# Earlier splitting of two output projections' weight blocks, and three of each expert's loads in unequal pieces

## The reference

```python
for layer in range(2):
    # shift, scale and gate rows of each sublayer: silu(c) @ ada_w[layer] + ada_b[layer]
    hx, hc = modulate(x, ...), modulate(ctx, ...)
    if layer == 0:
        yx, yc = fourier_window_mixer(hx, hc, mix_in_w, mix_out_w, win_sink, ...)
    else:                                     # no ctx output is needed
        yx, yc = diff_mixer(hx, hc, diff_qkv_w, diff_out_w, diff_lambda, diff_subln_g, ...)
    x = x + g1x * rmsnorm(yx)                 # ctx likewise in layer 0
    # layer 0: swiglu with 2816 hidden; layer 1: 8 experts of 3584 hidden, two per token
    x = x + g2x * rmsnorm(channel(modulate(x, ...)))
```

## Time and profile before

| | |
|---|---|
| time, median of 3 runs | 1702.79 us (1701.99 to 1703.03) |
| the profiled execution | 1705.14 us, of which 1703.4 us span |
| TensorE busy | 1620.9 us, 95% |
| VectorE, ScalarE busy | 525.9 us, 400.5 us |
| read from HBM | 471.36 MB, 277 GB/s over the span |
| chain that ended last | PE 89%, DVE 5%, DMA 2%, ACT 2%, SPq 1%, issue 1% |

### The profile page before, as it was taken

One profiled execution on the slowest core, in us unless ns is written; L12 is line 12 of the kernel. 1 busy time (PEld: TensorE's weight loads), 2 busy tenths in 40 slices (PEclk: granted clock), 3 DMA queues, 4 the chain that ended last, 5 costly groups with the idle time before them and its releaser, 6 DMA issues.

```text
span 1703.4 us, 31517 instructions
## 1 busy us (share of the span) xinstructions
PE 1620.9 (95%) x13979; PEld 970.4 (57%) x13979; DVE 525.9 (31%) x829; ACT 400.5 (24%) x724; POOL 34.4 (2%) x70
## 2 busy tenths in 40 slices
PE   5999889999999989997899999999999999999996
PEld 2855578878788877866644434454453444544432
DVE  3417367665533366357500010100101010020012
ACT  3227353211232253348300101011011100010101
POOL 1000100010000000000000000000000000000000
PEclk9999999999999999999799999999999999999998
DMA  9461725676623324103999999999999999999995
GB/s 368 175 195 60 252 77 174 197 254 231 217 91 122 113 80 134 40 0 133 362 377 374 378 408 408 413 406 411 408 409 411 394 411 405 410 412 399 410 397 226
DMA packets 140559, 474.61 MB, mean 279 GB/s; under 512 B 11176, under 2 KB 35144, under 8 KB 121984
## 3 DMA queue, kind: packets, MB, share of 16 engines
q1 hardware_dynamic: 137344, 467.64, 71.8%
q0 software_dynamic: 3072, 4.88, 1.0%
HBM read 471.36 MB, written 1.13 MB: 277 GB/s over the span
## 4 chain that ended last, share of the span: by engine, by line
PE 89%; DVE 5%; DMA 2%; ACT 2%; SPq 1%; issue 1%; DVEq 0%; ACTq 0%
PE ps L1139 85%; DMA w_raw<-in_ada_w_dram 1%; SPq L585 1%; DMA w_raw<-in_expert_out_w_dram 1%; PE ps L1644 1%; DVE w_lo L1759 1%; DVE work L1828 1%; PE ps L1322 1%; ACT p L953 0%; ACT w_hi L725 0%; DVE row_max L2094 0%; PE ps L1636 0%; DVE p L2120 0%; DVE h_t L1817 0%; DVE work L2026 0%
## 5 line engine op out<-in xcount | busy, mean ns | idle before, releaser
L1139 PE MATMUL ps<-w_hi,h_t 128*128 128x512 f32 (+1 forms) x960 | 295.9, 389 | 13.5 <-DVE h_t L1817 5.4
L1139 PE MATMUL ps<-h_t,w_hi 128*128 128x512 f32 (+1 forms) x768 | 223.3, 376 | 6.2 <-DVE h_t L1817 6.2
L1139 PEld LDWEIGHTS ps<-w_hi,h_t 128*128 128x128 f32 x960 | 181.6, 192 | 51.4 <-DVE w_lo L1942 4.1
L1759 DVE TENSOR_TENSOR w_lo<-w_raw,w_hi 128x2048 fp32r<-128x2048 f32 x57 | 130.6, 2292 | 219.3 <-ACT w_hi L725 219.0
L1139 PE MATMUL ps<-w_lo,h_t 128*128 128x512 f32 (+1 forms) x480 | 186.4, 388 | 0.0
L1139 PE MATMUL ps<-w_raw,h_te 128*32 128x512 f32 (+2 forms) x2224 | 178.4, 475 | 1.5 <-ACT silu_g L1053 0.8
L725 ACT ACTIVATE w_hi<-w_raw 128x2048 fp32r<-128x2048 f32 x57 | 109.0, 1914 | 290.2 <-PE ps L1139 289.8
L1139 PE MATMUL ps<-w_moe,h_te 128*32 128x512 f32 (+2 forms) x2256 | 170.5, 456 | 0.0
L1139 PEld LDWEIGHTS ps<-h_t,w_hi 128*128 128x128 f32 x768 | 142.0, 192 | 33.8 <-issue 9.2
L1139 PE MATMUL ps<-work 128*32 128x512 f32 (+6 forms) x1232 | 147.7, 485 | 8.3 <-ACT p L953 3.7
L2282 DVE TENSOR_TENSOR residual<-silu_g,ps 128x512 f32<-128x512 f32 (+1 forms) x20 | 12.4, 621 | 438.5 <-ACT silu_g L1056 418.0
(11 more groups left out here) (285 smaller groups left out, 1281.2 us busy)
## 6 DMA issues: line engine op xcount, KB each, us to landing
w_raw<-in_expert_in_w_dram SPq DMA_DIRECT2D x68, 1024.0 KB, 18.8
w_moe<-in_expert_in_w_dram SPq DMA_DIRECT2D x62, 1024.0 KB, 18.6
work<-in_expert_in_w_dram SPq DMA_DIRECT2D x53, 1024.0 KB, 18.2
w_raw<-in_ada_w_dram SPq DMA_DIRECT2D x48, 1024.0 KB, 5.4
w_raw<-in_expert_out_w_dram SPq DMA_DIRECT2D x37, 1024.0 KB, 17.9
w_moe<-in_expert_out_w_dram SPq DMA_DIRECT2D x36, 1024.0 KB, 18.2
work<-in_expert_out_w_dram SPq DMA_DIRECT2D x33, 1024.0 KB, 17.9
w_raw<-in_ffn_in_w_dram SPq DMA_DIRECT2D x44, 512.0 KB, 5.0
```

Of the source, the lines that this page charges most:

```text
L1139: return pe.matmul(out_, l, r, start=first, stop=last, skip_group_check=True)
L1759: dve.tensor_tensor(WLO[:, b % SPL, :], WRAW[:, slot_w[b], :], WHI[:, b % SPL, :].bitcast(F32), ALU.subtract).then_inc(lo_done, 1)
```

## The change

Three groups of edits:

1. `raw_order` takes blocks 5 and 6 directly behind block 4. ScalarE and VectorE split block 5 before they wait for block 3's product, and block 6 before they wait for block 4's; nothing is split in the units of the first attention. VectorE's `ada_rows(2)` moves behind `output0(15)`.
2. Blocks 54 and 55 are split while TensorE works on the last column group of q, k, v (n = 5); nothing is split in the units of the second attention. The heads of tile 0 are transposed (banks 2 and 3) ahead of the probabilities of unit 15, and ScalarE evacuates them in unit 14; the values of unit 15 move into the output projection, before its third row group; the heads of tile 1 go to banks 4 and 5. SP issues expert loads 5 to 8 first, without waiting for the scores.
3. The second output block of each of an expert's first three steps (b = 1: 3 of its 42 loads, 24 in all) is loaded by three transfers, of partitions 0 to 111, 112 to 119 and 120 to 127. Each raises the semaphore by 16, and TensorE waits for all three.

```diff
-    raw_order = [("ada", a) for a in range(8)] + [("w", r) for r in range(5)]
-    raw_order += [("ada", a) for a in range(8, 20)] + [("w", 5), ("w", 6)]
-    raw_order += [("ada", a) for a in range(20, PE_ADA)] + [("w", r) for r in range(7, B_FFNIN + 3)]
+    raw_order = [("ada", a) for a in range(8)] + [("w", r) for r in range(B_MIXOUT + 2)]
+    raw_order += [("ada", a) for a in range(8, PE_ADA)] + [("w", r) for r in range(B_MIXOUT + 2, B_FFNIN + 3)]
...
+    def moe_uneven(n):
+        kind, s_, b = ROUND[n][:3]
+        return kind == "out" and s_ < STEPS - 1 and b == 1
+
     def moe_parts(n):
-        return 2 if ROUND[n][:2] == ("in", STEPS - 1) else 1
+        return 2 if ROUND[n][:2] == ("in", STEPS - 1) else 3 if moe_uneven(n) else 1
...
+    HEAD_BANK = (2, 4)
+    UNEVEN = ((0, P - 16), (P - 16, P - 8), (P - 8, P))
...
-                sp.dma_start(w, rows.rearrange("(p j) n -> p j n", j=2)).then_inc(done, 16)
+                rows = rows.rearrange("(p j) n -> p j n", j=2)
+                for lo, hi in UNEVEN if moe_uneven(n) else ((0, P),):
+                    sp.dma_start(w[lo:hi], rows[lo:hi]).then_inc(done, 16)
...
-                sp.wait_ge(scores, U0 + U1)
-                for n in range(RING0):
-                    if n == 3:
+                for n in [5, 6, 7, 8, 0, 1, 2, 3, 4] + list(range(9, RING0)):
+                    if n == 0:
+                        sp.wait_ge(scores, U0 + U1)
+                    elif n == 3:
                         sp.wait_ge(pv_done, U0 + U1)
...
         act.activation(F_N, ps[:, 0:4, :], ACT.Copy).then_inc(f_copied, 1)
+        hi_upto(B_MIXOUT + 1)
         act.wait_ge(used, B_MIXIN + 4)
...
         ins.then_inc(q_ctx, 1)
+        hi_upto(B_MIXOUT + 2)
         act.wait_ge(used, B_MIXIN + 5)
...
-            if u in (13, 15):
-                hi_upto(B_MIXOUT + (u - 11) // 2)
...
             hi_upto(min(B_QKV + 2 * n + 2 + SPL, B_DOUT))
+            if n == 5:
+                hi_upto(B_DOUT + 2)
             act.wait_ge(used, B_QKV + 2 * n + 2)
...
-            if 13 <= u < U1 - 1:
-                hi_upto(B_DOUT + u - 12)
...
-        act.wait_ge(lam_dve, 2)
-        heads_hi(0)
+            if u == U1 - 2:
+                act.wait_ge(lam_dve, 2)
+                heads_hi(0)
+
         output1(U1 - 1)
...
+            if u == U1 - 1:
+                pe.wait_ge(exps, U0 + U1 - 1)
+                head_transposes(0)
             pe.wait_ge(prob_scaled, U0 + u + 1)
...
-        head_transposes(0)
-        values1(U1 - 1)
-        linear(B_DOUT, ZT, [(0,), (1,)], range(0, 8, 2), before=heads_split, between={6: late_columns})
+        linear(B_DOUT, ZT, [(0,), (1,)], range(0, 8, 2), before=heads_split,
+               between={2: lambda: values1(U1 - 1), 6: late_columns})
...
```

More of the change, by code:

```diff
@@ L964, in output1, with heads_hi @@
                            accum_out=SS[:, u:u + 1]).then_inc(o_raw, 1)
+        def heads_hi(t):
+            for b in range(2):
+                act.wait_ge(o_tr, 2 * t + b + 1)
+                act.activation(ZT[:, 0, 4 * b:4 * b + 4, P * t:P * t + P],
+                               ps[:, HEAD_BANK[t] + b, :].rearrange("p (h q) -> p h q", h=4), ACT.Copy,
+                               scale=GSUB[:, 1:2]).then_inc(z_hi, 1)
         exps1(0)
@@ L1461, in values1, with head_transposes @@
             ins.then_inc(pv_done, 1)
+        def head_transposes(t):
+            for b_ in range(2):
+                pe.wait_ge(o_norm, 2 * t + b_ + 1)
+                for hh in range(4):
+                    h = 4 * b_ + hh
+                    ins = pe.transpose(ps[:, HEAD_BANK[t] + b_, hh * P:hh * P + P], OA[:, t, h * P:(h + 1) * P], ID[:])
+                ins.then_inc(o_tr, 1)
         for u in range(U1):
@@ L1475, in _ @@
                 values1(u - 1)
-        def head_transposes(t):
-            for b_ in range(2):
-                pe.wait_ge(o_norm, 2 * t + b_ + 1)
-                for hh in range(4):
-                    h = 4 * b_ + hh
-                    ins = pe.transpose(ps[:, 2 * t + b_, hh * P:hh * P + P], OA[:, t, h * P:(h + 1) * P], ID[:])
-                ins.then_inc(o_tr, 1)
         def late_columns():
@@ L1959, in _ @@
         lo_upto(B_MIXIN + 2 + SPL)
+        lo_upto(B_MIXOUT + 1)
         dve.wait_ge(used, B_MIXIN + 4)
@@ L1963, in _ @@
         dve.sem_inc(q_x, 1)
+        lo_upto(B_MIXOUT + 2)
         dve.wait_ge(used, B_MIXIN + 5)
@@ L2009, in _ @@
                 output0(u - 1)
-            if u in (13, 15):
-                lo_upto(B_MIXOUT + (u - 11) // 2)
+        output0(U0 - 1)
         ada_rows(2)
-        output0(U0 - 1)
         lo_upto(B_MIXOUT + 2 + SPL)
@@ L2079, in _ @@
                 lam_whole()
+            if n == 5:
+                lo_upto(B_DOUT + 2)
             dve.wait_ge(used, B_QKV + 2 * n + 2)
@@ L2108, in heads_lo @@
                 dve.scalar_tensor_tensor(out=ZT[:, 1, 4 * b:4 * b + 4, P * t:P * t + P],
-                                         in0=ps[:, 2 * t + b, :].rearrange("p (h q) -> p h q", h=4),
+                                         in0=ps[:, HEAD_BANK[t] + b, :].rearrange("p (h q) -> p h q", h=4),
                                          scalar=GSUB[:, 1:2],
@@ L2130, in _ @@
                 combine1(u + 1)
-            if 13 <= u < U1 - 1:
-                lo_upto(B_DOUT + u - 12)
             if u == 11:
```

## The result

| | median, us | ratio to before, 95% interval |
|---|---|---|
| before | 1702.39 (4 runs, 1701.57 to 1703.03) | |
| changed | 1824.38 (4 runs, 1813.88 to 1838.72) | 1.072 (1.0655 to 1.0785) |

The forecast was 1683.0 in a range from 1678 to 1700. The kernel is 122 us slower. That is the side of rival (a), and beyond its price.

A forecast was written before the change was run, and what follows sets the result against it. PE was taken as the bound, with DMA also full in the experts. Span 1703.4 - 8.3 - 6.0 - 5.5 = 1683.6 us, plus 1.7 around it 1685.3 as profiled, so median 1683.0; range 1678 to 1700.

The forecast's parts named there:

- rival (a): Uneven loads in the experts: narrow pieces slow the stream, costing 50 to 55 us, 1739 to 1743 in all; chance 15%.
- Part 1: End of the first attention: two PE waits shortened and the clock restored, 8.3 us saved, between 5 and 9.
- the terms (3.26, 2.0 and 1.3): Before the first output projection: wait for scaled probabilities 3.26 us, wait for the last `h_t` 2.0, clock on PE's work 1.3.
- the clock's term: From the last microsecond before 190 us to 196: full clock instead of 0.78 saves some 1.7 us.
- The assumption that it was to support: First attention's end: TensorE, kept fed, is not throttled, as in 130:176 us at clock 1.00; the clock terms rest on it.
- Part 2: End of the second attention: 4.83 + 3.0 - 1.3 - 0.5 = 6.0 us saved, between 3.5 and 7.
- the new wait of 1.3 us: Second output projection: PE waits for unit 15's values, evacuated and normalised, before tile 1's heads; 0 to 1.7 us, taken as 1.3.
- the 4.83 us: End of the second attention: PE's wait for VectorE's `p`, behind the splits of blocks 54 and 55, goes entirely.
- Part 3: Uneven expert loads: relieving eight DMA engines cuts PE's load waits in the tail by 5.5 us, between 0 and 6.8.
- I take the value of the shape nearest to the 112-partition piece, no penalty: Uneven expert loads: narrow pieces priced at zero, like a 128-partition piece at 379 to 440 GB/s, not 64 partitions at about 215.
- wide pieces of the next can fill what a narrow one leaves idle: Argument against rival (a): the queue holds several loads, so later wide pieces use what a narrow piece leaves idle.
- The relief: Expert loads: eight engines carry seven rows instead of eight, 7.7 us less each, offsetting instruction packets assumed on them.

The follow-up runs named there:

- the added loads: Six groups of full, narrow and strided loads, data thrown away, added on idle DMA engines to the changed kernel without uneven loads: 1689.07 us in one execution.
- parts 1 and 2 alone: The changed kernel with `moe_uneven` returning False, so no uneven loads, against the kernel before: 1689.56 us, ratio 0.9917.
- 112 and 16: The changed kernel with its 24 uneven blocks in two pieces, of 112 and 16 partitions, against the kernel before: 1811.36 us, ratio 1.0655.

## Why the prediction was wrong

- **Part 1, -8.3 us forecast.** Right in the time, 8.9, and a little over the high end of 9 between marks, 9.6. Ahead of the output projection's start 6.8 were gained where the terms (3.26, 2.0 and 1.3) make 6.6, and the wait is 0.70 for 0.7. Behind it 2.8 were gained, where the clock's term was 1.7. That the start of 181.09 is 1.2 earlier than the forecast 182.3 is luck: in that execution the first transposes already start 1.0 sooner (122.78 for 123.80). One row was misread: in 130:176 PE is busy 43.56 of 46 us, and 46.00 is the length of the stretch. The assumption that it was to support held all the same, with 13.30 of 14 us busy at clock 1.00. The dip a tenth of the way in isn't in the slices of the earlier trace rows either, which have one near the middle; it is the 0.85 and 0.78 of the earlier trace rows. The splits were hidden: VectorE's idle time of 7.19 us is 4.76 now, the split inside it.

```profile
85.74 2.29 DVE L1770 TENSOR_TENSOR w_lo<-w_raw,w_hi 128x2048 fp32r<-128x2048 f32 x1
92.79 0.35 DVE L1929 TENSOR_TENSOR work<-ps,tables 128x64 f32<-128x64 f32 x2 [4.76 <-PE ps L1148]
```

- **Part 2, -6.0 us.** Right: 5.6 in the time and 6.8 between marks; the new wait of 1.3 us is 1.30. The forecast of no wait for `p` came true for the 4.83 us; one of 1.06 stayed.
- **Parts 1 and 2 count in full** at the end: right. Alone they make 1689.56; the forecast's terms make 1688.5.
- **Part 3, -5.5 us.** Wrong, by 140 us. The step that failed is "I take the value of the shape nearest to the 112-partition piece, no penalty". The only rows of a transfer with fewer than 128 partitions said half the rate, and the 112-partition piece was put on the other side because its number is near 128. It runs at 0.76 of the rate by itself, 0.7 us too slow, and the two small pieces got no term at all in the sum, though by themselves they cost up to 1.8 us. I had worked out 0.6 us a block as the point from which the sum turns. In the stream the measured term is 5.6 us a block, 135 us in all, in place of a gain of 5.5.
- **Rival (a)** had the mechanism and the sign, at 15%, and a price of 2.1 to 2.3 us a block. Alone the pieces measure up to 2.5, so the size was right for idle engines, by luck: it took the rate of 64 partitions for the whole megabyte, but 112 partitions lose much less than that (0.7) and the small pieces the rest. In the stream it is 5.6, and the rate fell to 351 GB/s, not to the 380 that I gave as its sign. What I set against it, "wide pieces of the next can fill what a narrow one leaves idle", is the opposite of what happened: whole loads are slowed too (5711 slow packets, at most 3072 of them in uneven blocks).
- **The relief** rested on a cause (instruction packets on certain engines) that the rows only allowed. That cause stays unshown; what the added loads do show is that a transfer of 8 partitions ends with eight completions (and one update at its issue) and one of 112 with 16, as the sum took it. The most that the tail offered was 6.8 us against a known risk of 50, so even a fair chance of (a) made part 3 a bad bet.

The version that beats both kernels is parts 1 and 2 alone, 1689.56 us.

## What to carry to other kernels

Where the DMA engines are the second limit, a transfer is a choice of partitions before it is a number of bytes. Cut a load by columns, or into even and odd partitions; here every cut that had a run of neighbouring partitions, 24 blocks of it, cost 5.1 to 5.7 us a block, and small strided pieces 1.4 to 1.7. Price a new shape by the nearest row that has its property (fewer than all partitions), not its size, and when the gain is capped by a small wait and the loss by a whole stream, take the loss as the forecast unless a row excludes it. A saving ahead of a stream that follows PE counts in full.

## What the runs showed of the hardware

- Two interleaved halves of 64 partitions run at the full 406 GB/s in the stream, two contiguous halves at 338 over a stage where they make one load in fourteen.
- Small strided pieces aren't free either: 64 + 32 + 16 + 16 partitions at strides of two, four, eight and eight cost 1.4 us a block, where 64 + 64 at a stride of two costs nothing.
- The changed kernel's executions spread over 1.4% (1813.88 to 1838.72), those of before beside them over 0.1%. The other kernels with all 24 blocks in runs of neighbours spread too (1801.69 to 1823.72 with 112 and 16). Why is open.
- The engines of one load drift apart also without uneven loads: with parts 1 and 2 alone, the first and the last completion of a load lie up to 3.2 us apart in the first two experts and 6.3 to 9.6 us in the last four.
